# A two-layer trunk kernel: a spilled expert split over four column tiles, state-space lags loaded by whole partitions, and each layer's fifth expert loaded ahead

## What is computed

```python
for i in range(DEPTH):                      # DEPTH = 2
    hn = rms_norm(h, norm_mix[i])
    mix = chunked_rel_attention(...) if i % 2 == 0 else s5_mixer(...)
    h = h + mix
    hn = rms_norm(h, norm_ffn[i])
    h = h + hierarchical_moe(hn, ...)       # top group of 4, then top 2 of its 8 experts
return rms_norm(h, norm_final)

# hierarchical_moe, t: (256, 1024), gates: (256, 32) with two entries a row
for e in range(32):
    hid = silu(t @ w_gate[e]) * (t @ w_up[e])          # 1024 -> 256
    out = out + gates[:, e:e+1] * (hid @ w_down[e])     # 256 -> 1024

# s5_mixer: 64 groups of 16 channels, each with a 64-dim complex diagonal state;
# y = Re(C x) + D u, then gelu, then a * sigmoid(g) with [a, g] = y @ w_out
```

## Time and profile before

| | |
|---|---|
| median of 3 runs | 858.52 us |
| time of the profiled execution | 859.13 us |
| its span in the trace | 857.4 us |
| TensorE (PE) busy | 687.7 us, 80% |
| VectorE (DVE) busy | 189.6 us, 22% |
| ScalarE (ACT) busy | 127.2 us, 15% |
| GpSimd (POOL) busy | 189.6 us, 22% |
| bytes moved | 256.13 MB, mean 299 GB/s |
| mean granted TensorE clock | 0.911 of full |

### The profile page before, as it was taken

How to read it: one execution, slowest core, us unless ns; L and a number is a source line. 1 busy time by engine, 2 the same in 40 slices (tenths; PEclk the granted TensorE clock), 3 DMA queues, 4 the chain that set the end, 5 groups by cost and what they waited for, 6 DMA issues and landing times.

```text
span 857.4 us, 12011 instructions
## 1 busy us (share of the span) xinstructions
PE 687.7 (80%) x5209; PEld 410.3 (48%) x5209; DVE 189.6 (22%) x421; ACT 127.2 (15%) x274; POOL 189.6 (22%) x234
## 2 busy tenths in 40 slices
PE   7999989898898886895553859998789979577564
PEld 4778877564453454462321444445454435244231
DVE  2131331442032120021032190135002202001004
ACT  1043233120010110011010212012201101001001
POOL 3000301525995920510884000000000000000000
PEclk9999999999898898897875989999989989899787
DMA  9986222758996999999999885234599799999981
GB/s 309 346 215 201 99 99 86 290 97 364 421 422 258 425 421 419 422 421 422 419 256 119 202 260 222 98 117 202 217 421 420 311 423 419 421 421 420 421 372 50
DMA packets 73721, 256.13 MB, mean 299 GB/s; under 512 B 15536, under 2 KB 45328, under 8 KB 47168
## 3 DMA queue, kind: packets, MB, share of 16 engines
q1 hardware_dynamic: 70816, 246.27, 75.9%
q0 software_dynamic: 2064, 7.93, 3.1%
q10 hardware_dynamic: 784, 1.09, 0.7%
HBM read 249.02 MB, written 5.20 MB: 297 GB/s over the span
## 4 chain that ended last, share of the span: by engine, by line
PE 47%; DMA 35%; DVE 7%; SPq 4%; issue 3%; ACT 2%; POOL 2%; DVEq 0%; ACTq 0%; POOLq 0%
DMA ring<-in_moe_w_down 16%; DMA ring<-in_moe_w_up 10%; PE ps L1538 8%; PE ps L1558 7%; PE ps L1733 7%; PE ps L1435 5%; PE ps L1307 5%; PE ps L1371 3%; DMA ub<-xn 3%; DMA ring<-in_moe_w_gate 3%; PE ps L1310 3%; PE ps L1569 2%; DMA ring<-in_attn_w_qkv 1%; DMA chunk_inputs<-stage 1%; SPq L351 1%
## 5 line engine op out<-in xcount | busy, mean ns | idle before, releaser
L1538 PE MATMUL ps<-ring,xg 128*32 128x256 f32 x2048 | 143.4, 443 | 60.8 <-DMA ring<-in_moe_w_gate 32.4
L1538 PEld LDWEIGHTS ps<-ring,xg 128*32 128x32 f32 x2048 | 82.9, 127 | 128.8 <-issue 104.9
L1558 PE MATMUL ps<-ring,hidT 128*32 128x512 f32 x528 | 80.1, 716 | 29.2 <-DMA ring<-in_moe_w_down 23.9
L1288 PE MATMUL ps<-ident,ones 128*128 128x512 f32 x108 | 53.6, 652 | 20.3 <-issue 17.4
L1109 DVE TENSOR_TENSOR hid<-sg,ps 128x256 f32<-128x256 f32 (+1 forms) x18 | 7.6, 420 | 245.2 <-ACT sg L814 245.2
L1569 PE MATMUL ps<-y_sb,pickT 128*128 128x512 f32 x128 | 59.0, 604 | 2.8 <-DVE y_sb L1118 2.8
L1307 PE MATMUL ps<-xnT,ring 128*128 128x256 f32 x256 | 57.6, 382 | 2.4 <-DMA ring<-in_attn_w_qkv 1.7
L1435 PE MATMUL ps<-pick,xn 128*128 128x256 f32 x256 | 58.6, 383 | 0.2
L1733 PE MATMUL ps<-ring,yT 128*128 128x512 f32 x128 | 56.3, 595 | 2.4 <-ACT yT L879 1.8
L1558 PEld LDWEIGHTS ps<-ring,hidT 128*32 128x32 f32 x528 | 20.2, 128 | 77.0 <-issue 69.0
L1307 PEld LDWEIGHTS ps<-xnT,ring 128*128 128x128 f32 x256 | 47.8, 190 | 10.4 <-issue 2.4
(11 more groups left out here) (297 smaller groups left out, 716.6 us busy)
## 6 DMA issues: line engine op xcount, KB each, us to landing
ring<-in_moe_w_down SPq DMA_DIRECT2D x66, 1024.0 KB, 19.0
ring<-in_moe_w_gate SPq DMA_DIRECT2D x66, 1024.0 KB, 18.1
ring<-in_moe_w_up SPq DMA_DIRECT2D x66, 1024.0 KB, 18.5
ring<-in_attn_w_qkv SPq DMA_DIRECT2D x11, 1024.0 KB, 12.0
ring<-in_ssm_w_out SPq DMA_DIRECT2D x8, 1024.0 KB, 11.5
ring<-in_attn_w_o SPq DMA_DIRECT2D x4, 1024.0 KB, 5.7
ring<-kernel_lags SPq DMA_DIRECT2D x8, 512.0 KB, 22.2
chunk_inputs<-stage POOLq DMA_DIRECT2D x3, 1024.0 KB, 9.2
```

The costliest lines, as they stand in the source:

```text
L1288: mm(ps[:, bank, :], ones[:], ident[:].unsqueeze(1).to_broadcast([P, 4, P]), start=True, stop=True)
L1538: ins = mm(ps[CAP * h:CAP * (h + 1), GUB, F * half:F * (half + 1)], p.xg[:, c, CAP * (ROUND * r + h):CAP * (ROUND * r + h + 1)], w, start= ...
L1558: ins = mm(ps[CAP * h:CAP * (h + 1), DNB + b, :], hidT[:, r, j, CAP * h:CAP * (h + 1)], w, start=(j == 0), stop=(j == FT - 1), tile_positi ...
```

## The change

Four things change together.

1. The spill pass uses all four column tiles: tile h computes a quarter of the hidden columns (64 of 256) for gate and up, and a quarter of the output columns (256 of 1024) for down, for the same 32 tokens. `pick_o` is repeated four times; `y_sb` is cleared first and filled as four blocks on its diagonal, two by ScalarE and two by VectorE.
2. The lags are loaded by four transfers of 128 partitions, one for each ring slot. The order of m in the partitions is turned round, so `uq` is copied from `ub[:, ::-1]` and `apw` is read unreversed.
3. `WARM["state-space norm"]` is 6 instead of 20.
4. Expert 4 of each layer is loaded ahead of the layer (`load_ahead`) into memory of its own (`ahead_gu`, `ahead_d`), which lies over the chunk tables. Ring slot 0 then takes the fullest expert in octet 0's second round, and octet 1 loads experts 9 to 11 while slot 0 waits for the spill pass, as before, for expert 8. For room `disc` and `b_raw` move; the load of `b_raw` waits for `logit_done`, and `chunk_outputs` waits for octet 0's second round before it writes over the ahead weights.

The diff, cut:

```diff
-WARM = {"start": 6, "norm": 7, "choice": 5, "ranks": 2, "state-space norm": 20, "loads": 0}
+WARM = {"start": 6, "norm": 7, "choice": 5, "ranks": 2, "state-space norm": 6, "loads": 0}
...
-        pick_o = fixed("pick_o", [P, TT, CAP])
+        pick_o = fixed("pick_o", [P, TT, ROUND, CAP])
...
-        disc = at("disc", [ST, 12, P], 13856)
+        disc = at("disc", [ST, 12, P], 17952)
+        ahead_gu = [at("ahead_gu0", [P, GU], 13856), at("ahead_gu1", [P, GU], 8736)]
+        ahead_d = [at("ahead_d0", [P, MAT], 11808), at("ahead_d1", [P, MAT], 8736 + GU)]
...
-                sp.wait_ge(S.first_done, k0 + 1)
-                next_round(0, 1)
                 sp.wait_ge(count_ready, layer + 1)
                 fullest = sp.value_load(count_i[0:1, 2 + layer:3 + layer], min_val=0, max_val=E - 1)
...
+                for n in range(2):
+                    first = ROUND if n == 0 else OCT
+                    sp.wait_ge(S.first_done, k0 + n + 1)
+                    if n == 0:
+                        gate_up(layer, fullest, 0, 0, slot_full[0])
+                    for s in range(1, RING):
+                        gate_up(layer, first + s, s, 0, slot_full[s])
+                    sp.wait_ge(S.gu_done, k0 + n + 1)
...
+            def load_ahead(layer):
+                e = E * layer + ROUND
+                for half, w in enumerate((wg, wu)):
+                    sp.dma_start(ahead_gu[layer][:, half * MAT:(half + 1) * MAT], w[:, e, :]).then_inc(ahead_full, 16)
+                sp.dma_start(ahead_d[layer][:], wd[:, e, :]).then_inc(ahead_full, 16)
...
+            sp.wait_ge(o_evac, HP)
+            sp.wait_ge(k_stored, 16 * (Q - 1))
+            load_ahead(0)
             experts(0)
...
-            for m in range(Q):
-                sp.dma_start(ring[GC * m:GC * (m + 1), :, GU:SLOT],
-                             k_dram[:, Q - 1 - m:2 * Q - 1 - m, :].rearrange("c (s l) n -> c s (l n)", l=2)).then_inc(toe_loaded, 16)
+            for s in range(RING):
+                lags = bass.AP(tensor=k_dram.tensor, offset=2 * s * D, ap=[[D, Q], [(2 * Q - 1) * D, GC], [1, 2 * D]])
+                sp.dma_start(ring[:, s, GU:SLOT], lags).then_inc(toe_loaded, 16)
...
             for s in range(RING):
                 down(1, s, s, down_full[s])
+            load_ahead(1)
             experts(1)
...
                 for i in pairs:
+                    if i == 1:
+                        pool.wait_ge(main.down_done, 2)
+                    if i == 2:
+                        pool.wait_ge(main.gu_done, 2)
...
+            pool.wait_ge(logit_done, 1)
...
             def moe_dve(p, after):
                 S, rows = p.S, slice(0, p.rows)
+                wide = F // ROUND if p.spill else F
+                if p.spill:
+                    V.memset(y_sb[:, 0, :], 0.0)
                 if after and not after.spill:
                     make_pick(after, after.octet)
...
                 def gate_up(r, half, done):
+                    if p.spill:
+                        n = F // ROUND
+                        for c in range(KT):
+                            for h in range(ROUND):
+                                w = ring[:, 0, half * MAT:(half + 1) * MAT].rearrange("p (c f) -> p c f", c=KT)
+                                ins = mm(ps[CAP * h:CAP * (h + 1), GUB, n * half:n * (half + 1)], xg_o[:, c, :],
+                                         w[:, c, n * h:n * (h + 1)], start=(c == 0), stop=(c == KT - 1), tile_position=(0, CAP * h))
+                        ins.then_inc(done, 1)
+                        return
...
+                    for j in range(FT if p.spill else 0):
+                        for h in range(ROUND):
+                            w = ring[:, 0, GU:SLOT].rearrange("p (j d) -> p j d", j=FT)[:, j, 256 * h:256 * (h + 1)]
+                            ins = mm(ps[CAP * h:CAP * (h + 1), DNB, 0:256], hidT[:, r, j, 0:CAP], w,
+                                     start=(j == 0), stop=(j == FT - 1), tile_position=(0, CAP * h))
```

More of the change, by code:

```diff
@@ L157, in trunk_program @@
         c_raw = at("c_raw", [P, 2, KT, 2, NS], 9760)
-        b_raw = at("b_raw", [P, 2, ST, GC], 11808)
+        b_raw = over("b_raw", [P, 2, ST, GC], xnT_at)
         wbt = over("wbt", [P, 8, 2, Q, GC], xnT_at)
@@ L259, in __init__ @@
                 self.units = 1 if self.spill else 4
-                self.rows = CAP * tiles
+                self.rows = P
                 self.xg = xg_o if self.spill else xg
@@ L1117, in moe_dve @@
                     dve.wait_ge(S.down_done, p.k + r + 1)
-                    V.tensor_scalar(y_sb[rows, r, 512:D], ps[rows, DNB + 1, :], p.gslot[rows, r:r + 1], None, ALU.mult)\
-                     .then_inc(S.yl_done, 1)
+                    if p.spill:
+                        for h in (2, 3):
+                            part = slice(CAP * h, CAP * (h + 1))
+                            ins = V.tensor_scalar(y_sb[part, r, 256 * h:256 * (h + 1)], ps[part, DNB, 0:256], gslot_o[part, 0:1],
+                                                  None, ALU.mult)
+                        ins.then_inc(S.yl_done, 1)
+                    else:
+                        V.tensor_scalar(y_sb[:, r, 512:D], ps[:, DNB + 1, :], p.gslot[:, r:r + 1], None, ALU.mult)\
+                         .then_inc(S.yl_done, 1)
                 if after:
@@ L1529, in loaded @@
                         return
-                    for s in range(p.tiles):
+                    here = p.layer is not None and not p.spill and (p.octet, r) == (0, 1)
+                    if here:
+                        pe.wait_ge(ahead_full, 48 * (p.layer + 1))
+                    for s in range(1 if here else 0, p.tiles):
                         first = 16 if s == 0 and full is not slot_full else 0
@@ L1534, in gate_up @@
                 def gate_up(r, half, done):
+                    if p.spill:
+                        n = F // ROUND
[6 more added lines that the diff above has]
+                        return
                     for c in range(KT):
                         for h in range(p.tiles):
-                            w = ring[:, h, half * MAT:(half + 1) * MAT].rearrange("p (c f) -> p c f", c=KT)[:, c, :]
+                            w = ring[:, h, 0:GU]
+                            if h == 0 and p.layer is not None and not p.spill and (p.octet, r) == (0, 1):
+                                w = ahead_gu[p.layer]
+                            w = w[:, half * MAT:(half + 1) * MAT].rearrange("p (c f) -> p c f", c=KT)[:, c, :]
                             ins = mm(ps[CAP * h:CAP * (h + 1), GUB, F * half:F * (half + 1)],
@@ L1739, in unit @@
                         pe.sem_inc(slot_free[s], 1)
-            pe.wait_ge(toe_loaded, 16 * Q)
+            pe.wait_ge(toe_loaded, 16 * RING)
             own_chunk(0)
```

82 lines of the change are left out of this document (48 added, 34 removed).

## The result

The changed kernel takes **845.62 us** (median of 4 runs, 843.27 to 847.78); the kernel before took 858.80 beside it (median of 4 runs, 858.01 to 861.92). The ratio is 0.984, with an interval of 0.981 to 0.987: 1.6% faster, and 19 us slower than the prediction, outside its range. The profiled execution took 847.04 us, with a span of 845.3.

A forecast was written before the change was run, and what follows sets the result against it. Expert stages were taken as bound by full DMA engines, with losses at the spill pass and between the layers; -6.9 - 19.4 + 2 - 7.8 = -32.1 from 859.13 gave 827.0, 826.4 against the median; range 819 to 838.

The forecast's parts named there:

- The lag loads: Between the layers: new form at 421 GB/s, 10 us; uq copied at 457 instead of 483.28, -19.4 us new.
- Rival (c): New lag loads use half the engines: 210 GB/s, 20 us, ub some 2 us later, kernel 828.5; chance 0.13.
- The restarts: Round (1,1) loads start earlier in both expert stages: -6.9 us in layer 0, -7.8 in layer 1.
- The spill pass: Expert stages on four tiles: layer 1 gate and up 7.09 to 3.5 us, down 3.62 to about 1.0.
- The clock: Full clock in octet 1's first gate half, 3.7 us; low clock at the mixer's start costs +2 us (0 to 5).
- rival (a): Clock falls after the new spill pass anyway, or a fetch stall hits its burst: +4.3 us, 830.7; chance 0.18.
- rival b: GpSimd takes layer 0's gain: pick comes late or the queue runs dry, +5.5 us, 832; chance 0.12.
- The branch: Between the layers: TensorE's idle before the warming products falls from 17.44 to some 5 us.
- rival d: Branch stall stays at 17 us, TensorE ready at 462, warm: +2 to +4 us, 829.5; chance 0.05.
- Twenty to six: Fewer warming products between the layers save nothing by themselves, as the wait is over sooner.

The follow-up runs named there:

- by_lag: The changed kernel with kernel_lags stored in DRAM by lag and then channel, so each load is 128 evenly spaced rows; 825.28 us, ratio 0.957.
- plain_source: The changed kernel with the four lag loads reading experts' down matrices (128 partitions of 8 KB, outer dimension 128); 825.57 us, ratio 0.962.
- channel_first_source: The changed kernel with the two outer dimensions of the lag source exchanged, 16 x 8 x 2048, same overlapping rows; 829.32 us, ratio 0.966.
- split_only: The changed kernel without the expert loaded ahead, its loads in the order of before; 854.16 us, ratio 0.996.
- ahead_only: The changed kernel with the old spill pass on one column tile, expert 4 still loaded ahead; 862.67 us, ratio 1.004.
- by_lag_warm20: The kernel with lags stored by lag and channel, with 20 state-space norm warming products instead of 6; 837.32 us, ratio 0.972.

## Why the prediction was wrong, point by point

**The lag loads, the step that failed.** "I take the destination as the cause and the new form at 421 GB/s". I compared the new form with the expert loads by destination and bytes per partition, and took as equal what differed: the source's outer dimension, 8 instead of 128. Measured: 125 GB/s and `uq` at 485.39 instead of 457. The term was to be -19.4; `uq` came 5.1 us later after the issue of the lags than before, and the whole stretch changed by +0.7. by_lag, the same bytes from a source counted plainly, and plain_source are about 20 us faster, so what I wrote of the steps behind the loads (who is late next, how soon `uq` follows) holds within some us.

**Rival (c)** had the cause, at a chance of 0.13, and the wrong price. It let half of the engines carry half of the rate, 210 GB/s; measured 125. And it let `ub` come 2 us later, where it came with the end of the lags, 33 us after its issue. Half the engines were not the price: all sixteen give 223 GB/s in channel_first_source. I had bounded the rate from above only; the earlier trace rows gave 115 GB/s as the lower end, for a transfer whose share was full. With that end the lags end at 434 + 36.5 = 470.5, `uq` comes at about 473, and the same sum gives 842. If `ub` has to share that rate, as it did, 5 MB take 45.6 us, `uq` comes at about 480, and the sum gives 849; the measured 845.62 lies between.

**The restarts.** Issue of round (1,1), counted from that of (0,1): layer 1 predicted -7.8, measured 64.5 against 73.1, -8.6. Layer 0 predicted -6.9, measured 71.2 against 77.5, -6.3. The -6.9 holds a slip: its terms (1 for the gather, 2.6 for the down product, 2.6 for the clock) make 6.2, and octet 1's start should have been 261.8, not 261.1. The nearness is in part luck: the gather started 2.4 us earlier instead of 1, and octet 1 started 3.6 earlier, with the 2.6 of the clock as forecast. The rule behind both ("how much earlier this `first_done` comes, as long as the queue drains before it. [...] The spill pass must follow") is what split_only and ahead_only show. The restart itself took 12.5 us instead of 13.9, which I had kept fixed; hence 9.8 in layer 1 as a whole.

**The spill pass.** Gate and up 3.5 predicted, 1.99 measured (128 records, 15.5 ns a record). The term was mis-sized by its row: the earlier trace rows has products of 128 columns, these have 64. In layer 1 the gap of 1.00 us brought it to 3.3 from first to last, near the 3.5 by luck. Down 1.0 predicted, 1.07 measured. Clearing `y_sb` 0.91, within 0.3 to 2.

**The clock** in octet 1's first product is full in both layers, as forecast; rival (a) is out. At the mixer's start +2 us was forecast for a low clock. The turn of `uq` did take 1.5 us more, but no loss is left at the end of that work: from the turn to the first product of the output projection 25.0 us pass in the changed kernel and 25.1 in by_lag, 27.2 in by_lag_warm20 with a full clock, and 29.6 before. Before, the clock was full for the turn and fell behind it (`s_in` 3.40 us instead of 2.04). So no row bears the term out; what makes these stretches differ is not shown.

**GpSimd (rival b).** `pick` took 4.23 us instead of 2.90 in layer 0, and the queue was to stay full by 2.4 us. In the changed kernel it does (410 GB/s from 287 to 290). In by_lag the same stretch runs at 360 and the next 3 us at 248 GB/s, in split_only at 156, and layer 0 as a whole takes 241.4 and 242.3 instead of 239.1. Of the ten kernels with both edits seven took 240.9 to 241.5. So the margin is about nothing, and some 2 us go back in most executions.

**The branch (rival d).** TensorE's idle time before the warming products fell from 17.44 to 6.40, predicted 5.

**Twenty to six.** "Save nothing by themselves, as the wait is over sooner": true only while the lags are slow. On my own forecast (`uq` at 457, twenty products until about 464 even from 445 on) they would have been in the way. It is worth 9 us of the stretch between the layers.

**Ahead of layer 0** 3.3 us were lost (197.6 against 194.3), which no step foresaw. In the ten kernels with both edits that stretch takes 194.8 to 197.9 (mean 196.1), in the four others 193.7 to 194.9. Part of it arises before the new loads are issued (the second `w_o` load at 67.32 instead of 66.76, the third at 94.42 instead of 93.01). No run tells the cause.

## What to carry to other kernels

A transfer's rate is not read from its destination and its bytes alone: compare how both sides are counted out in their slowest dimension, and if the row that you price from differs there, take the slowest comparable row as a bound. Where a stage is bounded by loads and by compute in turn, shortening one of them may give nothing; price the two together, by which of them ends last at the restart. A filler that hid in a wait has to be costed against the wait that is left.

## What the runs showed of the hardware

The first three rows are 1 MB transfers of 8 KB a partition (in by_lag as two runs of 4 KB), the last one 512 KB transfers of 32 KB a partition. Rates are of windows of 4 us or more.

| outer dimension of the source | destination | DMA share | GB/s |
|---|---|---|---|
| 128 rows | 128 partitions | 0.95 to 1.03 | 390 to 430 |
| 16 blocks of 8 | 128 partitions | 1.0 | 223 to 240 |
| 8 blocks of 16 | 128 partitions | 0.5 | 111 to 158 |
| 16 rows | 16 partitions | 0.94 to 1.09 | 107 to 127 |

With the share, this reads as: 8 blocks go over 8 engines, 16 blocks over 16. The Trainium skill's page "DMA: Bandwidth & Descriptors", section "Why a DMA increments its semaphore by 16 and not by 1", gives that number (the largest up to 16 that divides both sides' slowest dimensions); by that rule 8 and 16, and the shares agree.

It does not give the rates, since 223 GB/s at a full share is half of 420. An explanation that fits: engine number e writes partitions 8e to 8e+7 (or 16e to 16e+15) in turn, so at any moment the engines write to partitions that lie 8 (or 16) apart. The Trainium skill's page "SBUF — State Buffer", section "Door 1: The DMA port swizzle", gives a port by bits 2, 3, 4 and 6 of the partition's number. By it partitions 16 apart reach four ports (about 109 GB/s) and partitions 8 apart eight (about 218). The measured 125 and 223 are near both, but the 156 to 158 of split_only are well over four ports. So the engines don't step strictly together, if this is the explanation at all; no run shows it.

TensorE's wait behind the untaken branch goes with the loads that run beside it, not with their bytes. At a full share it is longer the slower they are: 17.44 us before and 18.4 with the old destination, 12.4 and 12.1 at 223 GB/s, 7.7 to 8.7 at about 400. At half the share it is the shortest, 6.4 to 6.6, though the lags run at their slowest. That would fit code that is fetched over engines which the lags leave free; no run shows it.
